# Expert weights as whole-matrix transfers of 2 MB, other row caps for the expert blocks, and small blocks that split their output columns over the two halves of the TensorE array

## The reference

```python
h2 = rmsnorm(x, norm2_g)
eidx, gates = hier_route(h2, ...)     # top-1 of 4 groups, then top-2 of its 8 experts
# for every expert e and the rows that chose it:
h = jax.nn.silu(xb @ w1[e]) * (xb @ w3[e])    # w1, w3: 1024 x 512
out = h @ w2[e]                               # w2: 512 x 1024
x = x + segment_sum(out * gate, token)        # two experts for each token
y = rmsnorm(x, normf_g)
```

## Time and profile before

| what | value |
|---|---|
| median of 3 runs | 1024.66 us (1024.5 to 1025.6) |
| the profiled execution | 1025.62 us, span of its instructions 1024.0 us |
| mean granted TensorE clock | 0.957 |
| PE busy | 921.0 us (90%) |
| DVE, ACT, POOL busy | 247.6, 111.0, 157.4 us |
| HBM read, written | 234.55 MB, 24.60 MB |
| q1 (SP), q0 (GpSimd) | 47740 packets with 238.54 MB, 10144 packets with 18.95 MB |

### The profile page before, as it was taken

The page is one execution under the profiler, slowest core; times in us unless marked ns, Lnnn a source line. Parts: engine busy times, 40 slices in busy tenths (PEclk is TensorE's granted clock), DMA queues, the critical chain, the costliest instruction groups (busy, mean ns, idle before and its releaser), DMA issues. The chain is left out here.

```text
span 1024.0 us, 24939 instructions
## 1 busy us (share of the span) xinstructions
PE 921.0 (90%) x10522; PEld 587.5 (57%) x10522; DVE 247.6 (24%) x760; ACT 111.0 (11%) x172; POOL 157.4 (15%) x239
## 2 busy tenths in 40 slices
PE   5999999999999973999999999989988999898940
PEld 2545545455455542876777677657556685674620
DVE  1434452454534553410000000000000000000006
ACT  0211110111101110001010101010010010010004
POOL 1000000000000002112222222212112122112110
PEclk9999999999999995999999999999989999998985
DMA  8760010100101063999999999999999999999938
GB/s 340 277 251 21 22 41 0 41 21 21 41 0 43 39 247 98 394 366 390 363 387 363 370 367 369 368 372 376 368 390 375 379 384 380 355 389 363 326 70 322
DMA packets 57935, 258.22 MB, mean 252 GB/s; under 512 B 11410, under 2 KB 12490, under 8 KB 40853
## 3 DMA queue, kind: packets, MB, share of 16 engines
q1 hardware_dynamic: 47740, 238.54, 60.6%
q0 software_dynamic: 10144, 18.95, 8.1%
HBM read 234.55 MB, written 24.60 MB: 253 GB/s over the span
## 5 line engine op out<-in xcount | busy, mean ns | idle before, releaser
L1186 PEld LDWEIGHTS ps<-hT,big 128*64 128x64 f32 x8192 | 286.4, 138 | 40.1 <-issue 28.6
L1186 PE MATMUL ps<-hT,big 128*64 128x64 f32 (+8 forms) x8192 | 294.7, 233 | 14.7 <-DMA big<-in_exp_w 7.9
L1202 PE MATMUL ps<-big,poolT 128*64 128x512 f32 (+8 forms) x512 | 233.8, 609 | 11.3 <-DMA big<-in_exp_w 7.5
L1083 PE MATMUL ps<-big,hT 128*128 128x512 f32 x384 | 169.9, 602 | 3.3 <-DMA big<-in_w_in 1.9
L1202 PEld LDWEIGHTS ps<-big,poolT 128*64 128x64 f32 (+8 forms) x512 | 75.1, 152 | 145.8 <-issue 135.2
L985 DVE TENSOR_TENSOR poolT<-u,ps 128x256 f32<-128x256 f32 (+8 forms) x32 | 15.1, 472 | 505.1 <-PE ps L1186 467.4
L1083 PEld LDWEIGHTS ps<-big,hT 128*128 128x128 f32 x384 | 73.2, 193 | 94.6 <-issue 88.5
L545 POOL DMA_INDIRECT x_rows<-xn,sidx x32 | 49.4, 1545 | 385.3 <-ACT xn L695 363.3
L695 ACT ACTIVATE xn<-ps,gslot 64x1024 f32<-64x1024 f32 (+8 forms) x32 | 35.5, 1110 | 456.0 <-PE ps L1202 240.8
L525 POOL DMA_INDIRECT slot_table<-ids,dest x18 | 18.7, 1038 | 328.2 <-DVE dest L807 271.9
L1140 PE MATMUL ps<-big,yT 128*128 128x512 f32 x128 | 56.4, 593 | 0.9 <-DVE yT L874 0.9
(11 more groups left out here) (168 smaller groups left out, 469.1 us busy)
## 6 DMA issues: line engine op xcount, KB each, us to landing
big<-in_exp_w SPq DMA_DIRECT2D x192, 1024.0 KB, 25.9
big<-in_w_in SPq DMA_DIRECT2D x4, 1536.0 KB, 13.5
big<-in_w_out SPq DMA_DIRECT2D x2, 2048.0 KB, 14.9
x_rows<-xres SPq DMA_DIRECT2D x8, 512.0 KB
h_rows<-xn SPq DMA_DIRECT2D x8, 512.0 KB, 2.7
big<-x_rows SPq DMA_DIRECT2D x8, 512.0 KB, 7.3
out_y_prompt<-big SPq DMA_DIRECT2D x8, 512.0 KB, 2.9
xres<-in_x_prompt SPq DMA_DIRECT2D x1, 3072.0 KB, 11.1
```

The costliest lines, as they stand in the source:

```text
L1083: last = pe.matmul(ps[0:m, bank, :], hT[:, k, 0:m], win[:, k, part * AW:(part + 1) * AW], start=(k == 0), stop=(k == KD - 1))
L1186: last = pe.matmul(out[c * w:(c + 1) * w, j, 0:m], up_weights(n)[:, k, j * P + c * w:j * P + (c + 1) * w], xT[:, 4 * half + k, 0:m], start ...
L1202: last = pe.matmul(ps[0:m, 5 + cols, :], hhT[:, 2 * half + k, 0:m], down_weights(n)[:, k, cols * 512:(cols + 1) * 512], start=(half + k == ...
```

## The change

Three things change together. The weights of an expert come in three transfers (CH = 3, CHW = 4096): w1, w3 and w2 whole, 2 MB each, in 6 buffers of 16 KB a partition; w1 and w3 are then 16 KB in one piece for a partition, w2 four pieces of 4 KB, row p of every group of 128 rows on partition p as before. The counts in the waits follow. CLASSES has four ranges instead of five: pair 10 goes from (80, 68) to (84, 64), pairs 11 and 12 from (80, 68) to (80, 76), pairs 13 to 15 from (76, 72) to (80, 76); with it SMALL goes from 72 to 76. And in blocks with m up to 64 (s = 1 of pairs 1 to 10) w2's second 512 output columns go to PSUM partitions 64 and up of bank 6, so that the two column halves stand on different halves of the array; ACT then scales only the first 512 columns and DVE the other 512.

```diff
-CLASSES = ((1, 4, (96, 56)), (4, 7, (88, 64)), (7, 10, (84, 64)), (10, 13, (80, 68)), (13, 16, (76, 72)))
+CLASSES = ((1, 4, (96, 56)), (4, 7, (88, 64)), (7, 11, (84, 64)), (11, 16, (80, 76)))
 SMALL = max(c[1] for _, _, c in CLASSES)
-CH = 6
-CHW = 2048
+CH = 3
+CHW = 4096
...
+def in_halves(m):
+
+    return m <= NS
...
             def chunk_src(e, c):
-                half = c % 2
-                if c < 4:
-                    w = (exp_w1, exp_w3)[c // 2]
-                    return w[0, e].rearrange("(p k) n -> p (k n)", k=KD)[:, half * CHW:(half + 1) * CHW]
-                return exp_w2[0, e, half * 2 * P:(half + 1) * 2 * P, :].rearrange("(k p) n -> p k n", p=P)
+                if c < 2:
+                    return (exp_w1, exp_w3)[c][0, e].rearrange("(p k) n -> p (k n)", k=KD)
+                return exp_w2[0, e].rearrange("(k p) n -> p k n", p=P)
...
                     pool.wait_ge(sidx_ready, count)
+                    if in_halves(m):
+                        pool.wait_ge(y_half_ready, h)
                     pool.wait_ge(y_ready, count)
                     scatter_add(ys[s][0:m, :], sidx[s][0:m, :], rows_out[s])
...
                     act.wait_ge(gate_in[s], 16 * h + 16)
+                    if in_halves(m):
+                        act.activation(ys[s][0:m, 0:512], ps[0:m, 5, :], ACT.Copy,
+                                       scale=gslot[s][0:m, 0:1]).then_inc(y_ready, 1)
+                        continue
...
                     if not (final and s):
                         take_xgT(b + 1, caps_of[1 - s])
+                    if in_halves(m):
+                        dve.wait_ge(rows_out[s], 16 * h)
+                        dve.wait_ge(gate_in[s], 16 * h + 16)
+                        dve.wait_ge(used, CH * b + CH)
+                        dve.tensor_tensor(ys[s][0:m, 512:D], ps[NS:NS + m, 6, :],
+                                          gslot[s][0:m, 0:1].to_broadcast([m, 512]), ALU.mult).then_inc(y_half_ready, 1)
...
-                    for half in range(2):
-                        n = CH * s + 4 + half
-                        pe.wait_ge(chunk_in[n], 16 * h + 16)
-                        for k in range(2):
-                            for cols in range(2):
-                                last = pe.matmul(ps[0:m, 5 + cols, :], hhT[:, 2 * half + k, 0:m],
-                                                 down_weights(n)[:, k, cols * 512:(cols + 1) * 512],
-                                                 start=(half + k == 0), stop=(half + k == 2))
-                        last.then_inc(used, 1)
+                    n = CH * s + 2
+                    pe.wait_ge(chunk_in[n], 16 * h + 16)
+                    for k in range(KF):
+                        for cols in range(2):
+                            first = NS * cols if in_halves(m) else 0
+                            last = pe.matmul(ps[first:first + m, 5 + cols, :], hhT[:, k, 0:m],
+                                             down_weights(n)[:, k, cols * 512:(cols + 1) * 512],
+                                             start=(k == 0), stop=(k == KF - 1), skip_group_check=True)
+                    last.then_inc(used, 1)
```

More of the change, by code:

```diff
@@ L275, in build @@
         y_ready = sem("y_ready")
+        y_half_ready = sem("y_half_ready")
         ov_free = sem("ov_free")
@@ L353, in chunk_src @@
             def chunk_src(e, c):
-                half = c % 2
-                if c < 4:
-                    w = (exp_w1, exp_w3)[c // 2]
-                    return w[0, e].rearrange("(p k) n -> p (k n)", k=KD)[:, half * CHW:(half + 1) * CHW]
-                return exp_w2[0, e, half * 2 * P:(half + 1) * 2 * P, :].rearrange("(k p) n -> p k n", p=P)
+                if c < 2:
+                    return (exp_w1, exp_w3)[c][0, e].rearrange("(p k) n -> p (k n)", k=KD)
+                return exp_w2[0, e].rearrange("(k p) n -> p k n", p=P)
             def chunk_dst(n, c):
-                return chunk[n] if c < 4 else chunk[n].rearrange("p (k n) -> p k n", k=2)
+                return chunk[n] if c < 2 else chunk[n].rearrange("p (k n) -> p k n", k=KF)
             sp.dma_start(xres[:, 0, :], xp[0:P, :]).then_inc(in_x0, 16)
@@ L406, in _ @@
             sp.dma_start(x3_rows[T:T + P, :], xg[1][:, :]).then_inc(trash_zeroed, 16)
-            for n in range(10, 2 * CH):
+            for n in range(2 * CH - 1, 2 * CH):
                 sp.dma_start(chunk_dst(n, n - CH), chunk_src(FIRST + 1, n - CH)).then_inc(chunk_in[n], 16)
@@ L459, in _ @@
             sp.wait_ge(out_b, NT)
-            for n in range(CH, 10):
+            for n in range(CH, 2 * CH - 1):
                 load_chunk(FIRST + 1, n)
@@ L688, in block_pair @@
                     b = 2 * h + s
-                    act.wait_ge(used, CH * b + 2)
+                    act.wait_ge(used, CH * b + 1)
                     act.activation(s1T[:, :, 0:m], up1[:, :, 0:m], ACT.Silu).then_inc(silu_done, 1)
@@ L983, in block_pair @@
                     dve.wait_ge(silu_done, b + 1)
-                    dve.wait_ge(used, CH * b + 4)
+                    dve.wait_ge(used, CH * b + 2)
                     dve.tensor_tensor(hhT[:, :, 0:m], s1T[:, :, 0:m], up3[:, :, 0:m], ALU.mult).then_inc(hhT_ready, 1)
@@ L1178, in block_pair @@
                     for part, out in enumerate((up1, up3)):
-                        for half in range(2):
-                            n = CH * s + 2 * part + half
-                            pe.wait_ge(chunk_in[n], 16 * h + 16)
[L1182 to L1189, removed]
-                            last.then_inc(used, 1)
+                        n = CH * s + part
+                        pe.wait_ge(chunk_in[n], 16 * h + 16)
+                        for k in range(KD):
+                            for j in range(KF):
+                                for c in range(SPLIT):
+                                    w = P // SPLIT
+                                    last = pe.matmul(out[c * w:(c + 1) * w, j, 0:m],
+                                                     up_weights(n)[:, k, j * P + c * w:j * P + (c + 1) * w],
+                                                     xT[:, k, 0:m], start=(k + j == 0),
+                                                     stop=(k == KD - 1), skip_group_check=True)
+                        last.then_inc(used, 1)
                     if not (final and s):
@@ L1224, in _ @@
                         for k in range(KD):
-                            last = pe.matmul(ps[:, 2 + m, :], xT[:, k, :], up_weights(2 * m + k // 4)[:, k % 4, :],
+                            last = pe.matmul(ps[:, 2 + m, :], xT[:, k, :], up_weights(m)[:, k, :],
                                              start=(k == 0), stop=(k == KD - 1))
@@ L1235, in _ @@
                             last = pe.matmul(ps[:, 5 + cols, :], hhT[:, k, :],
[L1236 removed]
+                                             down_weights(2)[:, k, cols * 512:(cols + 1) * 512],
                                              start=(k == 0), stop=(k == KF - 1))
```

## The result

The changed kernel takes 1069.01 us (median of 4 runs, 1067.65 to 1073.67) against 1025.13 us on the same chip: ratio 1.043, 95% interval 1.040 to 1.047, slower by 44 us. The profiled execution took 1068.02 us, its span is 1066.4 us. The direction was as forecast and the time lies in the range, but the change is 44 us where 105 were forecast.

The account below looks back on a forecast made before the run. The prediction took the scatter-gather-gates loop through q0 as the bound, already from 804 us before the change. +73 (pairs 1 to 10), +31 (11 to 14) and +5 (ends) make +109 on 1025.6: 1134, stated as 1130 us, range 1045 to 1175.

Parts of the forecast that it names:

- The loop as the bound: Expert stage: scatter, row gather, gate gather, y, next scatter through q0 set the pace, before from 804 us on.
- The 76-row gather: Queue q0, 15 pairs: 76 rows sit on 4 engines, 19 each, ahead of the gates, and lengthen the loop.
- step A: Loop step with the 76-row gather ahead of the small block's gates: 21.6 us in pairs 1 to 10, today's packets.
- step B: The pair's other loop step: 13.2 + 2.1 = 15.3 us in pairs 1 to 10 with today's packets.
- The first rival: Expert stage: long gathers count, long packets don't; +13, +5 and ends +3, 1047 us; chance 0.2.
- the price of the long packets: Queue q0: each row alternates with weight packets, averaging 0.46 instead of 0.26 us, +0.20 us a row.
- 45 and 63 rows in line: Rows on the worst engine per pair: 45 in pairs 1 to 10 (A 29, B 16), 63 in pairs 11 to 14.
- the relief: Queue q0: weights are queued only 37.0/C of the time, lowering 45.9 us a pair to 43.0 in pairs 1 to 10.
- Halves at nothing: w2 of ten small blocks: 3.4 us of TensorE saved each, 34 us together, all beside busy DMA and the loop.
- Coarse transfers at nothing: Weight stream: 2 MB buffers come free later, but several transfers stay queued and the last w2 lands as before.
- 0 to 6 us gained by longer packets: w1 and w3 stream: 16 KB packets gain 0 to 2% on two thirds of the bytes, hidden if the loop bounds.
- The faster rival: Expert stage: gates don't land behind the long gather, the loop stays hidden; about 1012 us; chance 0.09.

Follow-up runs that it names:

- e7: Changed kernel with the gather of the gates issued ahead of the gather of the rows, nothing else: 1046.17 us (ratio 1.021).
- e11: Changed kernel with caps that all divide by 16 and the gates' gather ahead of the rows': 1026.11 us (ratio 1.001).
- e13: Kernel before with the change's new CLASSES (and so SMALL = 76) alone: 1047.80 us (ratio 1.023).
- e10: Kernel before with the gates' gather ahead of the rows' and nothing else: 1025.65 us (ratio 1.001).
- e1: Changed kernel with SMALL = 80 instead of 76: 1055.29 us (ratio 1.030).
- e3: Kernel before with SMALL = 76 and nothing else: 1053.66 us (ratio 1.028).
- e6: Changed kernel with w1 and w3 in two pieces of 8 KB a partition, so 8 KB packets: 1053.88 us (ratio 1.029).
- e4: Kernel before with whole-matrix 2 MB transfers alone (16 KB packets, old CLASSES, no halves): 1050.97 us (ratio 1.025).
- e14: Changed kernel without halves, full-width w2 in all blocks: 1068.74 us (ratio 1.043).
- e12: Kernel before with caps that divide by 16, gates gathered ahead of rows, and halves in all 64-row blocks; 1 MB transfers: 1014.46 us (ratio 0.990).
- e5: Kernel before with whole-matrix 2 MB transfers alone, but w1 and w3 in 8 KB packets: 1030.09 us (ratio 1.0045).
- e9: Kernel before with caps that all divide by 16 alone, order of gathers as before: 1016.24 us (ratio 0.992).

## Why the prediction was right in direction and wrong in size

**The loop as the bound.** Right for the changed kernel: gates were to be waited for in "nearly all blocks, in total over 400 us", and were 29 times, 529 us, and the order alone gives back 23 of the 44 us (e7). It is not the whole bound (e7 against e11, e13). For the kernel before it was misread: from 804 us on y does wait for gates, but the DMA share is 1.02 and taking most of that wait away gains nothing (e10). Packets of q1 fell from 47740 to 38012, by 9,728 and not by 8,192. The other 1,536 are packets of 4 bytes, 16 for each of the 96 transfers that there are fewer (4437 before, 2901 after).

**The 76-row gather.** Right that it costs, and by how much. The divisor of the row count sets the length: 80 rows beat 76 (e1), and SMALL = 76 alone costs 28 us (e3). Whether it costs them through the loop alone or also through the stream's rate is open (e13). That a pair came out at 36.8 us (e13) where 36.9 were forecast is in part luck: step A's base was put at 20.0 us from its scatter to y, the late step that it was copied from, with gates of 76 rows, and measured 18.5; step B was put at 13.2 and measured 14.2. The first rival's sum for the caps, +22 us, came out at +23 (e13).

**The step that failed is the price of the long packets: "+0.20 us a row" times 45 and 63 rows in line, with weights there "37.0/C of the time"**, C being the length of the pair. It made 43.0 and 47.1 us of pairs that measured 39.0 and 39.2. Packets were put at +83 us (1130 less 1047). All that is not caps cost +21 (1069 less e13's 1048), of it the packets 15 (e6). Term by term, +73 us for pairs 1 to 10 measured +33, +31 for pairs 11 to 14 measured -1, +5 for the ends measured +10. Of the +31, 25 were this price, and the rest came from taking one pair of 40.8 us for all four late pairs, which took 39.4 before.

The price itself was right: alone, with 16 rows in line in each step, it gives 3.2 us, and e4 shows +3.4 and +2.8. What failed is its sum over steps that share the queue. In the changed kernel step A grew by 2.7 us over e13, where 29 rows with the relief were to give 3.9; step B changed by nothing (13.6 against 14.2), where 16 rows were to give 2.2; and the late pairs, with 63, became 1.9 us shorter than e13's. The signs tell the same: the DMA engines were to idle a sixth of the stage and idle next to nothing up to 844 us (share 0.99 and 1.00), the rate was to be near 320 GB/s and was 358 (327 from 844 us on), scatters of a pair were to lie 42 to 48 us apart and lie 39. TensorE, which was to idle a sixth too, idled 12, 18 and 8% of the three stretches. Gathers of 76 rows land after 15 to 20 us, within the 15 to 25 named.

Where it went can be seen in the trace. Stretches of 8 us in step B of four pairs, from some 5 us after the scatter, first the changed kernel, then e13 (last columns: clock, DMA share, GB/s):

```profile
617.00:625.00 8.00, 8.00 (x101) 4.20 (x101) 0.00 (x0) 0.00 (x0) 2.29 (x4) 0.92 0.72 209
656.00:664.00 8.00, 8.00 (x131) 4.95 (x131) 0.00 (x0) 0.00 (x0) 1.62 (x4) 1.00 0.95 314
693.00:701.00 8.00, 8.00 (x114) 4.62 (x114) 0.00 (x0) 0.00 (x0) 1.89 (x4) 0.97 0.90 290
731.00:739.00 8.00, 8.00 (x118) 4.67 (x118) 0.00 (x0) 0.00 (x0) 2.38 (x4) 1.00 0.93 295
```

```profile
601.00:609.00 8.00, 8.00 (x101) 4.34 (x101) 0.00 (x0) 0.00 (x0) 1.94 (x4) 1.00 1.04 319
639.00:647.00 8.00, 8.00 (x135) 5.03 (x135) 0.00 (x0) 0.00 (x0) 2.16 (x4) 1.00 1.04 327
...
714.00:722.00 8.00, 8.00 (x126) 4.75 (x126) 0.00 (x0) 0.00 (x0) 2.23 (x4) 1.00 1.04 341
```

There the weight queue runs dry just while scatter, rows and gates of step B are under way: share 0.72 to 0.95 against 1.04. Over all ten steps B of pairs 1 to 10 it is 0.71 to 0.94, in the ten steps A 1.01 to 1.06. Rows that find no weight packet have none to wait for, whatever its size. Queue q1 alone in the first of these stretches, changed kernel:

```profile
q1 hardware_dynamic: 129, 1.08, 38.5%
q0 software_dynamic: 248, 0.59, 33.5%
```

It runs dry since TensorE gives no buffer back: it waits 3.79 us for the 76-row gather to land, its w2 starts at 612.38 behind the y of the block before and takes 10.02 us, at a granted clock of 0.70 over these 10 us, for what takes 7.1, and until it ends no 2 MB buffer is free.

```profile
596.63 9.88 PE L1201 MATMUL ps<-hT,big 128*64 128x88 f32 x256
610.30 1.11 PE L1048 MATMUL ps<-ident,xg 76*128 76x76 f32 x8 [3.79 <-DMA xg<-h_rows,gidx]
612.38 10.02 PE L1217 MATMUL ps<-big,poolT 128*88 128x512 f32 x16 [0.97 <-issue]
```

SP issues a transfer at 606.7 and the next at 622.5. The relief was thus in the sum, but spread evenly over the pair; in truth the small idle share of the DMA falls almost wholly into step B, where q0 needs it. e4 shows the same in a late pair. Its step A of pair 13 lasts from the scatter at 929.98 to the landing at 940.7, 10.7 us, though its packets are long; in the kernel before that step, from 902.32, took 16.8. First e4, then before:

```profile
935.00:943.00 8.00, 8.00 (x126) 4.99 (x126) 0.00 (x0) 1.11 (x1) 1.00 (x1) 1.00 0.69 182
907.00:915.00 8.00, 8.00 (x152) 5.64 (x152) 0.00 (x0) 0.00 (x0) 1.04 (x1) 1.00 1.03 344
```

That the dry stretch saves step B its price rests on this coincidence and on e4's pairs 1 to 10, where the queue is full and the price is paid; no run removed it by itself. In the late pairs of the changed kernel the share in step B is low too, 0.85 to 0.91 in pairs 11 to 13; why they take 39.2 us, less than e13's 41.1, is not shown beyond that.

**Halves at nothing.** Right (e14, e12); in e12, where no loop is in the way, TensorE waits for the stream instead. **Coarse transfers at nothing.** Nearly: 5 us (e5). **0 to 6 us gained by longer packets.** Not seen in any run. **The faster rival** fell: gates land behind the long gather, and turning the order round gave 23 us (e7). The Trainium skill's rule on the number of engines (DMA: Bandwidth & Descriptors, "Why a DMA increments its semaphore by 16 and not by 1") foretold the direction of every run on row counts (e1, e3, e9); its table in "Bandwidth" rates larger transfers higher, and going from 1 to 2 MB gained nothing here, where 2 MB in 8 KB packets took 1.0045 of the time.

## What to carry to other kernels

Look for loops that pass through a shared DMA queue without moving much: a 4-byte gather that stands behind a big one can set the pace of a kernel whose DMA engines are 99% busy. For gathers and scatters pick row counts that 16 divides: that alone made this kernel 0.8% faster (e9). Issue the small transfer that something waits for ahead of the large one that nobody needs yet: worth 23 us in the changed kernel (e7), and nothing in the kernel before (e10), so before repairing a wait look whether the stream behind it is full. A price per queued row, measured alone, holds only while the other queue is full: once the loop is the bound, ask where the idle time falls before multiplying.

## What the runs showed of the hardware

Four rows decide: with gathers of 76 rows instead of 72 their step goes from 13.8 to 18.5 us, and those of 80 rows do not go that way (e9's steps in pairs 1 to 10, all caps multiples of 16, stay within 11.6 to 14.3 us). With the 76-row gathers the stream is slower at the same share of DMA time, 365 to 367 GB/s against 373 to 375 (e13 against before).

The two DMA queues alternate packet by packet. The packet records show it for a 68-row scatter: in pair 10 of the kernel before (issued at 804.6) rows start 5.16, 5.79, 6.41, 7.04 and 7.67 us after its start, with three more such series of starts beside them, which fits 4 engines; in e4 (issued at 829.6) one goes 5.20, 6.13, 7.05, 7.98. So a row follows a row after 0.63 and 0.93 us. The row takes 0.33 us of it, and the rest is near the 0.317 and 0.62 us of one weight packet of 8 or 16 KB. The longer packets cost the kernel 20 us of 1025 for the same bytes in the same number of transfers (e4 against e5).

TensorE's mean granted clock was 0.90 from 640 to 844 us of the changed kernel, where it idled 37 of 204 us, some 7 us a pair, against 0.97 before.
